# A decoder trunk on Trainium2: the gelus of two expert tiles as one ScalarE operation, on two PSUM banks in turn

## What is computed

```
q = (x @ w_q)                        # 8 heads, two halves of 128
s = q . sub_keys                     # 128 scores per head and half
top 16 of each half, sums of pairs, top 16 of those -> expert = i1 * 128 + i2, gates = softmax
h = gelu(x . u_tab[expert])          # 128 x 128 experts in the table
y = sum over chosen experts of gates * h * v_tab[expert]
```

## Time and profile before

| | us |
|---|---|
| three runs | 1814.58, 1816.03, 1816.36 |
| median | 1816.03 |
| the profiled execution, its own time | 1816.5 |
| its span, first to last instruction | 1814.7 |
| TensorE busy | 1776.7 |
| VectorE busy | 1389.0 |
| ScalarE busy | 1200.8 |
| GpSimd busy | 481.2 |

### The profile page before, as it was taken

How to read it: one execution, slowest core, us unless ns; L and a number is a source line. 1 busy time by engine, 2 the same in 40 slices (tenths; PEclk the granted TensorE clock), 3 DMA queues, 4 the chain that set the end, 5 groups by cost and what they waited for, 6 DMA issues and landing times.

```text
span 1814.7 us, 38629 instructions
## 1 busy us (share of the span) xinstructions
PE 1776.7 (98%) x13968; PEld 1516.8 (84%) x13968; DVE 1389.0 (77%) x2491; ACT 1200.8 (66%) x1649; POOL 481.2 (27%) x709
## 2 busy tenths in 40 slices
PE   8999999999999999999999989999999999999998
PEld 8787888899988888888887878888999888888886
DVE  8879989788878887444597799897888788874445
ACT  4687888888874444455546878888888644445454
POOL 0010122122223323545300101131222233235543
PEclk9999999999999999999999999999999999999999
DMA  8454655655545555766573546556555455557663
GB/s 258 153 201 165 195 188 185 196 179 183 183 132 182 177 173 181 242 192 191 163 222 126 208 161 197 177 197 193 185 181 182 136 173 174 184 181 237 195 193 120
DMA packets 95980, 333.20 MB, mean 184 GB/s; under 512 B 11680, under 2 KB 16032, under 8 KB 95648
## 3 DMA queue, kind: packets, MB, share of 16 engines
q1 hardware_dynamic: 88992, 317.51, 53.3%
q10 hardware_dynamic: 6912, 14.77, 2.7%
HBM read 328.20 MB, written 4.03 MB: 183 GB/s over the span
## 4 chain that ended last, share of the span: by engine, by line
PE 86%; DVE 7%; ACT 3%; issue 3%; DMA 1%; POOL 0%; ACTq 0%; DVEq 0%; POOLq 0%; SPq 0%
PE bank L1603 15%; PE bank L1605 15%; PE bank L1604 15%; PE bank L1552 12%; PE bank L1554 12%; PE bank L1553 12%; PE bank L1865 3%; ACT squares_unread L585 1%; DVE top_index_u L1247 1%; DVE top_values L1240 1%; PE bank L1675 1%; DVE half_tiles L956 1%; DVE topk_rest L1245 1%; ACT half_tiles L577 1%; DMA shifted_u<-x_kept 1%
## 5 line engine op out<-in xcount | busy, mean ns | idle before, releaser
L1552 PE MATMUL bank<-xt_half,half_tiles 128*128 128x256 f16 x2272 | 620.0, 273 | 10.1 <-ACT scores L806 4.7
L1554 PE MATMUL bank<-xt_half,half_tiles 128*128 128x256 f16 x2272 | 619.9, 273 | 0.0
L1553 PE MATMUL bank<-xt_half,half_tiles 128*128 128x256 f16 x2272 | 619.8, 273 | 0.0
L567 ACT ACTIVATE hi<-raw 128x1024 fp32r<-128x1024 f32 x312 | 330.4, 1061 | 419.8 <-PE bank L1605 375.9
L939 DVE TENSOR_TENSOR lo<-raw,hi 128x1024 fp32r<-128x1024 f32 x312 | 403.1, 1293 | 197.4 <-ACT hi L567 196.2
L956 DVE SCALAR_TENSOR_TENSOR half_tiles<-raw,to_half,half_tiles 128x1024 f16<-128x1024 f32 x280 | 357.5, 1277 | 91.8 <-ACT half_tiles L577 90.2
L544 POOL TENSOR_TENSOR w_split<-h,w_split 128x256 fp32r<-128x256 f32 x256 | 297.5, 1163 | 441.3 <-ACT w_split L864 416.6
L1603 PE MATMUL bank<-hi,w_split 128*128 128x512 f32 x1024 | 402.1, 393 | 0.0
L1605 PE MATMUL bank<-hi,w_split 128*128 128x512 f32 x1024 | 398.9, 390 | 0.0
L1604 PE MATMUL bank<-lo,w_split 128*128 128x512 f32 x1024 | 398.4, 389 | 0.0
L577 ACT ACTIVATE half_tiles<-raw,to_half 128x1024 f16<-128x1024 f32 x280 | 319.9, 1142 | 100.9 <-POOL to_half L537 100.5
(11 more groups left out here) (228 smaller groups left out, 1783.2 us busy)
## 6 DMA issues: line engine op xcount, KB each, us to landing
raw<-in_stream SPq DMA_DIRECT2D x592, 512.0 KB, 4.1
early_raw<-in_stream SPq DMA_DIRECT2D x8, 512.0 KB, 5.7
shifted_u<-x_kept ACTq DMA_DIRECT2D x16, 142.0 KB, 5.2
ln_g<-in_ln_p ACTq DMA_DIRECT2D x4, 512.0 KB, 6.8
ln_b<-in_ln_p ACTq DMA_DIRECT2D x4, 512.0 KB, 9.0
keys_sb<-in_keys_t ACTq DMA_DIRECT2D x2, 1024.0 KB, 6.9
x_kept<-x ACTq DMA_DIRECT2D x4, 512.0 KB, 3.9
x<-x_kept ACTq DMA_DIRECT2D x4, 512.0 KB, 6.6
```

Of the source, the lines that this page charges most:

```text
L567: nc.scalar.activation(hi[:, j, :], raw[:, j, :], ACT.Copy).then_inc(*hi_done.one)
L1552: mm(dst, weight(0, slot, k), xt[:, k, 0, :], start=k == 0, stop=False)
L1553: mm(dst, weight(0, slot, k), xt[:, k, 1, :], start=False, stop=False)
L1554: last = mm(dst, weight(1, slot, k), xt[:, k, 0, :], start=False, stop=k == KC - 1)
```

## The change

Two U tiles with the same scale (an even and the odd one behind it) accumulate in the two halves of one bank, and one gelu of 512 columns takes both. The pairs use banks 4 and 5 in turn; banks 6 and 7 aren't written by U tiles any more. `gelu_done` counts pairs and starts at 2, and all its waits are counted in pairs. TensorE waits for it, and for the copied scores, only before even tiles. ScalarE's gelu and the square behind it both stand after the odd tile; nothing but the next tile's high half stands after the even one.

```diff
-        gelu_done = signal("gelu_done", NK, primed=RING)
+        gelu_done = signal("gelu_done", NK // 2, primed=2)
@@ act, u_turn
-                        act.wait_ge(*tile_used(layer, U0 + b + 1))
-                        nc.scalar.activation(h[:, b * SEQ:(b + 1) * SEQ], ring_banks[j][:, 0:SEQ],
-                                             ACT.Gelu, scale=from_half[:, slot_of(f)])\
-                          .then_inc(*gelu_done.one)
-                        if f % 2 and (f + 7) // 2 < UNITS:
-                            square((f + 7) // 2)
+                        if f % 2:
+                            act.wait_ge(*tile_used(layer, U0 + b + 1))
+                            nc.scalar.activation(h[:, (b - 1) * SEQ:(b + 1) * SEQ],
+                                                 ring_banks[j // 2][:, :], ACT.Gelu,
+                                                 scale=from_half[:, slot_of(f)])\
+                              .then_inc(*gelu_done.one)
+                            if (f + 7) // 2 < UNITS:
+                                square((f + 7) // 2)
@@ dve
-                dve.wait_ge(*gelu_done(layer, SEG))
+                dve.wait_ge(*gelu_done(layer, SEG // 2))
...
-                dve.wait_ge(*gelu_done(layer, NK))
+                dve.wait_ge(*gelu_done(layer, NK // 2))
@@ pe, u_tile
-                    pe.wait_ge(*gelu_done(layer, RING * i + (j - RING + 1)))
-                    half_tile(j, ring_banks[j][:, 0:SEQ])
+                    if j % 2 == 0:
+                        pe.wait_ge(*gelu_done(layer, 2 * i + (j // 2 - 1)))
+                    half_tile(j, ring_banks[j // 2][:, j % 2 * SEQ:(j % 2 + 1) * SEQ])
@@ pe, first turn
-                    pe.wait_ge(*s_done(layer, TT * (SCORE_GROUPS - 2) + j + 1))
+                    if j % 2 == 0:
+                        pe.wait_ge(*s_done(layer, TT * (SCORE_GROUPS - 2) + j // 2 + 1))
@@ pe, before the V stage
-                pe.wait_ge(*gelu_done(layer, NK - 2))
+                pe.wait_ge(*gelu_done(layer, NK // 2 - 1))
```

More of the change, by code:

```diff
@@ L555, in _ @@
             act.wait_ge(*consts_made(0, 1))
-            for _ in range(RING):
+            for _ in range(2):
                 act.sem_inc(gelu_done.sem, 1)
```

## The result

The changed kernel takes 1818.63 us (median of 12 runs, 1814.84 to 1821.15), the kernel before, run beside it, 1814.87 (12 runs, 1813.66 to 1818.33). The ratio is 1.0017, with a 95% interval of 1.0009 to 1.0025: between 1.6 and 4.5 us slower, 3.8 at the medians. The forecast, 1817.5, lies 1.1 us from the time, but part of that is luck. It was +1.5 on a median of 1816.03 from three runs; more runs of the kernel before put it 1.2 lower, and the measured step is 3.8 at the medians, above the band of +0.6 to +2.8 that the forecast gave for it.

The account below looks back on a forecast made before the run. TensorE, busy 98% of the span, was taken as the bound. Delays of 0.52 + 0.22 = 0.74 us per layer, +1.5 for two, other parts 0, on the median 1816.03 gave 1817.5 us; range 1814.0 to 1820.9.

Parts of the forecast that it names:

- Sizes of the gelu: ScalarE: a 512-column gelu takes 0.57 us between starts, about 680 ns long; 18 us less busy time, worth nothing by itself.
- Part 3: U tiles 2 and 3: TensorE's wait for the scores goes, but VectorE's work takes it over; costed at 0.
- Part 2: U stage: TensorE waits for the later square in four places per layer; 0.74 us per layer, +1.5 in all.
- step (e): Ahead of the gate matrices at 354.16: the odd gelu lies in the chain TensorE waits for; +0.22 us per layer.
- (b): Product at 283.15: GpSimd's wait ends 0.08 later, the wider gelu adds 0.22, so it comes 0.30 us later.
- (c): Loop through the square, 15.91 us a round, becomes 16.13; TensorE's start at 299.53 moves to +0.52.
- (d): Round from 299.53 to 315.31: TensorE had up to 0.56 us of room, 0.22 is used; nothing added.
- Step (a): Tile at 274.44, at the exp: two wide gelus replace three narrow ones in ScalarE's unbroken stretch; +0.08 us.
- The loop that gets longer everywhere: Rival: each of 20 preparations waiting for GpSimd between 183 and 350 hands 0.22 us to TensorE; 1820.8 us, chance 0.10.
- The scores' wait: Rival: TensorE keeps what its removed wait for the last scores cost; 1811.6 or 1812.8 us, chance 0.08.
- all was absorbed: Rival: 512 columns come at the cheap end or GpSimd's waits shift favourably; 1816.0 within 0.6 us, chance 0.26.
- The rule of the Trainium skill: Cycling through PSUM banks can swing the clock, so two could be worse than four; its rival 1820.9 us, chance 0.04.

Follow-up runs that it names:

- e9: Kernel before with only the wait for the last scores removed ahead of U tiles 2 and 3, which go to banks 0 and 1; 1814.00 us, ratio 0.9997.
- e1: Changed kernel with 20 and 16 unread small products filling TensorE's two pauses ahead of the first gate matrices; 1815.25 us, ratio 1.0004.
- e2: Changed kernel with TensorE's waits for the copied scores put back as in the kernel before, still two banks; 1815.95 us, ratio 1.0009.
- e6: Kernel before with 20 and 16 small products in the two pauses ahead of the first gate matrices; 1812.80 us, ratio 0.9992.
- e3: Changed kernel, still two banks, with each pair's gelu taken as two operations of 256 columns; 1820.22 us, ratio 1.0030.
- e5: Kernel before, four banks and gelus of 256, with only the even tile's gelu moved behind the odd tile's products; 1820.38 us, ratio 1.0029.
- e7: Kernel before with the square sums of odd tiles ahead of the odd gelu from the exp's turn on; 1811.49 us, ratio 0.9984.
- e10: Kernel before, unchanged, profiled once more; 1818.01 us in one run.
- e4: Changed kernel with the square sums of odd tiles moved ahead of the pair's gelu; 1814.94 us, ratio 1.0002.

## Why the prediction came out as it did

**Sizes of the gelu.** Right: 0.57 between starts, 675 ns. ScalarE saved 21.2 us where 18 were forecast, of no consequence.

**Part 3, cost 0.** Right by the trace (8.15 in both layers) and by e9. The clock fall of layer 1 went too, and was worth nothing, as read from rows 6.

**Part 2, step (e).** Right for the chain: 0.21 in e1 against 0.22. What the step put at nothing without a reason is the clock. The prediction calls the U stage gapless but for the scores and the exp; at the gates TensorE stood still for 1.14 us and then, 16 small products later, for another 0.96 (at 355.76), which no step names. With 0.21 more in front, the clock fell there in three layers of four, at 1.5 to 1.7 us each; e1 shows that with products in the pauses it doesn't. Why it stays up behind the same pauses in e2 is open.

**Steps (b), (c) and (d).** Between the tile at 274.3 and the product at 283.3 the changed kernel loses 0.28 (8.99 us against 8.71), up to 299.89 another 0.21, where 0.22 and 0.22 were forecast. The fourth stretch, which holds (c) and (d), is 0.21 longer in layer 0 and 0.18 in layer 1: one gelu passed, then nothing more.

**Step (a), mis-sized.** Forecast +0.08. From U tile 1 to the tile of the exp the distance is 93.5 us against 93.1 before, though the ScalarE stretch that the step counts behaves: from the preparation that waits for GpSimd (260.59 after, 260.71 before) to the table load (268.77 and 268.82) it grows by 0.07. The loss lies ahead of it: that preparation is already 0.5 us late against the end of tile 1. Nothing in TensorE's timeline shows it there, since TensorE still had room (63.73 against 63.80 to the product at 253). I had looked for places where TensorE waits and not at the lag of the line behind it, which is handed over whole as soon as the room ends. So the first three stretches cost 0.75 per layer where 0.30 was forecast.

**The sum.** The chain cost was forecast at 0.74 per layer, 1.5 in all; it is 1.2 and 2.4 (e1 against e6: 2.45). To this comes what each gained from filler: 3.4 in the changed kernel (the clock at the gates, and some of it may be the wait at layer 1's start), 2.0 in the kernel before. 2.4 + 3.4 - 2.0 = 3.8, but that sum can't fail, since it is made of the same four medians as the step; what stands by itself is the 2.3 of the stretches against the 2.45 of the medians. That 1817.5 came within 1.1 us of the time is in part luck: the base was 1.2 too high and the cost 2.3 too low. The gate matrices came 1.2 us later against U tile 1, not 0.7.

**The rivals.** The loop that gets longer everywhere did not come: the fourth stretch, 70 us with many such waits, costs 0.2. The scores' wait was not won. Not all was absorbed. The rule of the Trainium skill that the prediction sets against the change ("TensorE: Matmul & The Clock Gate", section "A second HAM failure mode: psum-queue depth-cycling") is not borne out: e3 with two banks and e5 with four are equally slow, and in their profiles the clock falls at both gates in the four-bank one and at neither in the other. Where it falls, the pauses come from VectorE's tables.

**What stays open.** Why the line ahead of the exp loses 0.25 to 0.4 us more per layer in the changed kernel than in e2, when TensorE doesn't stop at the scores. The order of before doesn't lose it (e9). One thing goes with it. In the profiles GpSimd's scale operation of one column takes either 0.19 us or over a microsecond; in the second of the two cases below it came first by a hundredth of a microsecond. Timelines of GpSimd and VectorE, first the changed kernel, then e2:

```profile
241.72 1.20 POOL L537 TENSOR_SCALAR to_half<-unit_bound 128x1 int32<-128x1 int32 x1
...
241.61 1.26 DVE L958 SCALAR_TENSOR_TENSOR half_tiles<-raw,to_half,half_tiles 128x1024 f16<-128x1024 f32 x1
```

```profile
241.99 0.19 POOL L537 TENSOR_SCALAR to_half<-unit_bound 128x1 int32<-128x1 int32 x1
...
242.00 1.28 DVE L958 SCALAR_TENSOR_TENSOR half_tiles<-raw,to_half,half_tiles 128x1024 f16<-128x1024 f32 x1
```

Where VectorE's rest of a tile has started, GpSimd stands until it ends; where GpSimd is first, it doesn't. The Trainium skill ("SBUF — State Buffer", section "Who interferes with whom") states this: a VectorE instruction with two SBUF inputs and a GpSimd instruction that reads SBUF exclude each other, and issue order decides. The trace agrees, 1.20 against 0.19 us. In all 28 layers profiled, the operation at this place (near 242 us in layer 0) is short where the stretch of tiles 2 and 3 takes 9.2 us or more (e2, e5, e7 and e10 among them) and long where it takes 8.15. Between e3 and e5, alike in their gelus, the first three stretches differ by 0.7 to 0.8 us, the longer ones with the long form; but the two differ in banks and in the wait for scores too. In the order of before the long form costs nothing, so it is not the whole cause, and I didn't test it alone.

## What to carry to other kernels

Price an operation that is moved in an engine's queue by what stands behind it, and not by what it saves. ScalarE had 21 us less work and the kernel became slower. The even tile's gelu had come to stand with the odd one, ahead of a square sum that the bottleneck waits for, and with four banks and narrow gelus that order alone (e5) cost as much. Look at a pause of TensorE twice, as a duration and as a risk to its clock. Look also at how late the line behind a wait runs where TensorE still has room: the 0.5 us lost there showed only at the exp. Then try the opposite order: the square ahead of the gelu in the kernel before gave 1811.5 us, the best here.

## What the runs showed of the hardware

**The clock can fall behind a pair of short pauses.** In the changed kernel 1.35 and 0.96 us, with 16 small products between, were followed by a granted clock of 0.50 in three layers of four. In e2 the same two pauses were not, in two layers; with 1.50 and 0.95 us the clock fell in both layers of e5 and in neither of e3. With 1.14 and 0.96 it fell in none of eight (the three profiles of before and e9). A single pause at the exp of 1.46 (after) or 1.67 us (before) left the clock at 1.00; behind one of 2.0 us (e4) it fell in both layers, and behind the 2.35 us at the scores in 12 of the 16 layers that have it. The Trainium skill ("TensorE: Matmul & The Clock Gate", section "HAM oscillation — how this bites in real kernels") tells of the clock falling in a single long wait for data between bursts of products; here it also fell behind two short waits with a little work between. Products of 128 columns that nobody reads kept it at 1.00 in both layers of e1, and the time was 3.4 us lower.

**A clock fall can be free.** At the scores it cost 1.27 us and all but 0.04 of it was back by the exp, a hundred microseconds on. At the gates it made the stretch 1.5 to 1.7 us longer, and the kernel without these falls (e1) was 3.4 us faster, so there it did not come back.
